# Second block's attentions: two PSUM banks in turn for the background products, one for the weighted sum over the keys

## The chip, the cores and the metric
The program runs on one core of one Trainium2 chip. The metric is the device time of one execution in microseconds (us); a profiled execution gives the trace from which rows are shown. The core has five engines that run their own instruction lists side by side and wait for each other by semaphores: TensorE (PE; its weight loads are listed as PEld), VectorE (DVE), ScalarE (ACT), GpSimd (POOL) and SyncE (SP, which issues the DMAs). Matmul results go to PSUM, which has eight banks of 128 x 512 float32; a bank can be written anew only when its last result has been copied out.

## The reference, cut to what matters
Two transformer blocks run one after the other over 512 tokens of width 1024. The second block has three branches, each an attention, gated and then merged:

```
q_a, k_a, v_a, ..., z_a, ..., gate_logits = split(h @ w_in)
o_a = top-k sparse causal attention   (8 heads of 64, 128 keys per query)
o_b = causal attention                (8 heads, 96 wide scores, 64 wide values)
o_m = attention over 256 memory rows  (4 heads of 128)
ys     = stack([o_a * silu(z_a), o_b * silu(z_b), o_m * silu(z_m)])
branch = einsum('nbsw,nwd->nbsd', ys, w_branch)
merged = einsum('bsnd,nbsd->bsd', sigmoid(gate_logits), branch)
x      = x + merged @ w_out
```

An attention is: scores = q k^T, softmax over the keys, then the sum over the keys of probability times value. z and the gate logits need only h, not the attention, so their products can run beside it.

## The kernel before, in words
Every float32 product of h or an activation with a weight tile is made of three 128x128 by 128x512 matmuls on high and low parts (`product`, lines 403 to 405). A weight tile (1024 x 128) is loaded by SP, its high part is written by ACT (`split_high`, L356), its low part by POOL (`split_low`, L365).

The kernel is a row of stages with a barrier between them. In the second block each branch makes a `Background` object (line 544): a list of jobs, one weight tile and one 128 x 512 output each (4 jobs for z, 8 for the gate, in the sparse branch 5 more for the latent branch's input). A job has 8 steps of 3 matmuls, so 24 matmuls. `Background.pe(pe, n)` puts the next n steps into PE's list, wherever a stage calls it; `Background.act` puts the copy of a finished job (`take`, L583) and the high part of a later weight tile (L356) into ACT's list, at the point where the next job begins. At a job's first step PE waits for its weight tile and, if an earlier job used the same bank, for that job's copy (`background_taken`). `bank(i)` names the bank: bank 7 for every job that begins inside another stage; the jobs from number `alone` on, which run by themselves in the stage after the attention (`finish`), take banks 0 to 6 in turn.

The background is called in these stages of the second block:
- `select_keys` (sparse branch; the top-k choice): after the last of 13 rotations PE does 36 background steps, 4 jobs and a half. The rotations use banks 4, 5 and 6 in turn; the last step of a rotation is ACT's copy L3075 (semaphore `rotated`).
- `rotate_tiles` (latent branch): one step after each of 16 rotations, whose banks are 0 to 3.
- `attend` (all three branches; line 2283): one step in each unit.

`attend` goes through units, one for each head and each 128 queries: 32 units in the sparse and in the latent attention (8 heads of 4, with 128, 256, 384 and 512 keys), 16 in the memory attention (4 heads of 4, 256 keys each). PE's list in unit i: the scores of unit i (L2307, banks 0 to 2), one background step (L403 to L405), the transposes of the probabilities of unit i-3 (L2318, banks 3 and 4), and, where i-4 is the last unit of a head, that head's weighted sum over the keys (L2332: 10 matmuls with causal keys, 8 of them in a row of the trace, 8 for the memory attention). The sum was put in bank 5 or 6 by the head's number. DVE scales, masks and takes the maximum (L2349, L2352) and divides by the sum (L2362, L2363); ACT takes the exponential (L2376), does its background part (L583, L356), copies the transposed probabilities (L2387) and a head's finished sum (L2394), in this order. The first block's attention calls `attend` too, with two value parts in banks 5 and 6 and no background.

Background jobs begin at units 4, 12, 20 and 28 of the sparse attention, at units 0, 8, 16 and 24 of the latent one, and at units 0 and 8 of the memory one.

Of the kernel before, what the change touches and what calls it, by code (L numbers as in the profile page):

```python
# [27 lines left out]
S = 512  # L28
# [515 lines left out]
class Background:  # L544
# [10 lines left out]

    def bank(self, i):

        return (i - self.alone) % 7 if i >= self.alone else 7

    def pe(self, pe, steps):  # L560
        k = self.k
# [1721 lines left out]
def attend(k, units, scale, background=Idle(), pace=0):  # L2283


    nc, G = k.nc, k.counter
    n = len(units)
    scored, maxed, expd, scaled = G("score_ready"), G("max_ready"), G("exp_ready"), G("prob_ready")
    turned, copied, summed, taken = G("turned_ready"), G("turned_taken"), G("sum_ready"), G("out_taken")
    NS, NB = 4, 3  # L2290
    TURN, SUM = 3, 4
    with ExitStack() as ctx:
        s = k.sbuf(ctx, k.fresh("scores"), [P, NS, S])
        pT = k.sbuf(ctx, k.fresh("probT"), [P, 2, max(un.keys for un in units) // P, S])
        small = k.sbuf(ctx, k.fresh("row_stats"), [P, NS, 4])

        with k.stage() as block:
            @block.tensor
            def _(pe):
                for i in range(n + SUM):  # L2300
                    if i < n:
                        un = units[i]
                        if i >= NB:

                            pe.wait_ge(*expd.ge(i - NB + 1))
                        for j, (q, key) in enumerate(un.pairs):
                            last = nc.tensor.matmul(k.banks[i % NB][:, 0:un.keys], q, key, start=(j == 0),  # L2307
                                                    stop=(j == len(un.pairs) - 1))
                        last.then_inc(*scored.inc())
                        background.pe(pe, pace)  # L2310
                    if 0 <= i - TURN < n:
                        m, un = i - TURN, units[i - TURN]

                        pe.wait_ge(*scaled.ge(m + 1))
                        if m >= 2:
                            pe.wait_ge(*copied.ge(m - 1))
                        for c in range(0, un.keys, P):
                            last = nc.tensor.transpose(k.banks[3 + m % 2][:, c:c + P], s[:, m % NS, c:c + P], k.const("ident"))  # L2318
                        last.then_inc(*turned.inc())
                    if 0 <= i - SUM and (i - SUM) % ST == ST - 1:  # L2320
                        m, h, un = i - SUM, (i - SUM) // ST, units[i - SUM]

                        pe.wait_ge(*copied.ge(m + 1))
                        heads = 2 // len(un.value)
                        if h >= heads:
                            pe.wait_ge(*taken.ge(h - heads + 1))
                        rows = slice(un.row, un.row + un.width)
                        for part, value in enumerate(un.value):
                            for c in range(un.keys // P):

                                q0 = 0 if un.mask is None else c * P
                                last = nc.tensor.matmul(k.banks[5 + (h % 2 if heads == 2 else part)][rows, q0:S], value(c),  # L2332
                                                        pT[:, h % 2, c, q0:S], start=(c == 0), stop=(c == un.keys // P - 1))
                        last.then_inc(*summed.inc())

            @block.vector
            def _(dve):
                chain = Chain(dve, G("dve_step"))
                for i in range(n + 1):
                    if i < n:  # L2340
                        un = units[i]
                        st = small[:, i % NS, :]
                        dve.wait_ge(*scored.ge(i + 1))
                        src = k.banks[i % NB][:, 0:un.keys]
                        if un.mask is not None:
                            if i >= NS:

                                dve.wait_ge(*turned.ge(i - NS + 1))
                            chain(nc.vector.scalar_tensor_tensor(out=s[:, i % NS, 0:un.keys], in0=src,  # L2349
                                                                 scalar=scale if un.scale is None else un.scale,  # L2350
                                                                 in1=un.mask, op0=ALU.mult, op1=ALU.add))
                            nc.vector.tensor_reduce(st[:, 1:2], s[:, i % NS, 0:un.keys], AX, ALU.max,  # L2352
                                                    negate=True).then_inc(*maxed.inc())
                        else:
                            chain(nc.vector.tensor_reduce(st[:, 0:1], src, AX, ALU.max))
                            nc.vector.tensor_scalar(st[:, 1:2], st[:, 0:1], -scale, None, ALU.mult).then_inc(*maxed.inc())
                    if i:
                        m, un = i - 1, units[i - 1]
                        st = small[:, m % NS, :]

                        dve.wait_ge(*expd.ge(m + 1))
                        chain(nc.vector.reciprocal(st[:, 3:4], st[:, 2:3]))  # L2362
                        nc.vector.tensor_scalar(s[:, m % NS, 0:un.keys], s[:, m % NS, 0:un.keys], st[:, 3:4], None,  # L2363
                                                ALU.mult).then_inc(*scaled.inc())

            @block.scalar
            def _(act):
                for i in range(n + SUM):
                    if i < n:
                        un = units[i]  # L2370

                        act.wait_ge(*maxed.ge(i + 1))
                        if i >= NS:
                            act.wait_ge(*turned.ge(i - NS + 1))
                        src = s[:, i % NS, 0:un.keys] if un.mask is not None else k.banks[i % NB][:, 0:un.keys]
                        nc.scalar.activation(s[:, i % NS, 0:un.keys], src, ACT.Exp, bias=small[:, i % NS, 1:2],  # L2376
                                             scale=1.0 if un.mask is not None else scale,
                                             accum_out=small[:, i % NS, 2:3]).then_inc(*expd.inc())
                        background.act(act, pace)
                    if 0 <= i - TURN < n:  # L2380
                        m, un = i - TURN, units[i - TURN]
                        h, t = m // ST, m % ST

                        act.wait_ge(*turned.ge(m + 1))
                        if h >= 2:
                            act.wait_ge(*summed.ge(h - 1))
                        nc.scalar.copy(pT[:, h % 2, 0:un.keys // P, t * P:(t + 1) * P],  # L2387
                                       k.banks[3 + m % 2][:, 0:un.keys].rearrange("p (c q) -> p c q", q=P)).then_inc(*copied.inc())
                    if 0 <= i - SUM and (i - SUM) % ST == ST - 1:
                        h, un = (i - SUM) // ST, units[i - SUM]  # L2390

                        act.wait_ge(*summed.ge(h + 1))
                        rows = slice(un.row, un.row + un.width)
                        nc.scalar.copy(un.out, k.banks[5 + h % 2][rows, :] if len(un.value) == 1 else  # L2394
                                       k.psum[:, 5:7, :]).then_inc(*taken.inc())

            @block.gpsimd
            def _(pool):
                k.split_low(pool, k.split_h)

            @block.sync
            def _(sp):
                k.prefetch_split(sp)
# [641 lines left out]
def select_keys(k, qk, qi, ki, wi, wiT, v, chosen, cos, sin, y, sg, gained_matrix, q_scale, background, fill):  # L3045

    nc, G = k.nc, k.counter
    norms_ctx = ExitStack()
    with norms_ctx, ExitStack() as ctx:
# [3 lines left out]
                      S, 2, room=sg, kept=(4, q_scale[:], AHD ** -0.5), sum_bank=3)  # L3053
        matrix, gained_cos = k.const("rotate_a"), sg[:, 7, :]

        items = [(x, matrix, cos) for x in (ki[:], *(qi[:, t, :] for t in range(4)))]
# [74 lines left out]
        with k.stage() as block:  # L3131
            @block.tensor
            def _(pe):
                for t in range(ST):
                    last = nc.tensor.matmul(k.banks[3][:, t * AH:(t + 1) * AH], wiT[:, t * P:(t + 1) * P],
                                            k.const("ident", AH)[:, 0:AH], start=True, stop=True)
# [16 lines left out]
                for i in range(FIRST, len(items)):  # L3153
                    fill.pe(pe, 4)
                    pe_rotate(pe, i)
                background.pe(pe, CHOOSE_STEPS)

            @block.scalar
# [538 lines left out]
```

## Time and profile before

| | us |
|---|---|
| Median of 3 runs | 1895.54 |
| Lowest and highest run | 1889.73, 1901.23 |
| The profiled execution | 1900.23 |
| Its span (first to last instruction) | 1898.4 |
| PE busy in it | 1746.5 (92%) |
| DVE, ACT, POOL busy | 880.0, 708.8, 726.5 |
| Mean granted TensorE clock | 0.946 of full speed |
| Sparse attention (stage) | 1227.05 to about 1345.5 |
| Latent attention | 1513.3 to about 1598 |
| Memory attention | 1732.4 to about 1768 |

The span is one execution's clock, from its first instruction; the profiled execution's time is 1.8 us more. A view by windows cuts the span at chosen times and gives each engine's busy time in each piece and PEclk, the clock that TensorE was granted: 1.00 is 2.4 GHz, 0.50 is 1.2 GHz, and a value between is a mixture over the piece. A timeline row is one instruction, or several alike in a row; in square brackets stands how long the engine had been idle before it and what ended the idle time.

### The profile page before, as it was taken

How to read it: one execution, taken by the hardware profiler on the slowest of the kernel's cores; microseconds unless marked ns; L12 is line 12 of the kernel's file. 1: busy time of each engine (PE TensorE's matmuls, PEld its weight loads, DVE VectorE, ACT ScalarE, POOL GpSimd, SP SyncE). 2: the span in 40 equal slices, each digit the busy share in tenths (PEclk: the TensorE clock that was granted, in tenths of full speed). 3: DMA queues.
4: the chain of work that ended last, by engine and by line, in shares of the span. 5: the costliest groups of instructions: out<-in, count | busy, mean ns of one | idle time of the engine just before them, and what ended most of it. 6: DMA issues, size and time to landing. Idle time of an engine off the chain costs nothing. (4 is left out here: it accounts for less than half of the span.)

```text
span 1898.4 us, 25330 instructions
## 1 busy us (share of the span) xinstructions
PE 1746.5 (92%) x10334; PEld 1305.1 (69%) x10334; DVE 880.0 (46%) x1448; ACT 708.8 (37%) x1195; POOL 726.5 (38%) x375
## 2 busy tenths in 40 slices
PE   5999998889998999999999997899998799987989
PEld 4866668858785878888788854644674466774777
DVE  4647884448524355333212938634142864314231
ACT  4334452234424432222233432334345155334431
POOL 5423433316440445555444543300244612452342
PEclk9999999879999999999999998967898899998999
DMA  4311120014320223322233311200113010341131
GB/s 165 136 56 56 56 68 4 4 57 123 107 93 23 89 78 101 100 89 94 84 101 106 132 45 34 67 22 14 43 53 109 23 34 17 128 139 60 51 106 56
DMA packets 39571, 138.55 MB, mean 73 GB/s; under 512 B 4384, under 2 KB 5664, under 8 KB 38304
## 3 DMA queue, kind: packets, MB, share of 16 engines
q1 hardware_dynamic: 39456, 136.93, 22.1%
q8 instruction: 82, 1.34, 0.3%
q14 instruction: 33, 0.27, 0.0%
HBM read 132.72 MB, written 4.19 MB: 72 GB/s over the span
## 5 line engine op out<-in xcount | busy, mean ns | idle before, releaser
L365 POOL TENSOR_TENSOR parts<-ring,parts 128x1024 fp32r<-128x1024 f32 (+3 forms) x251 | 572.4, 2285 | 962.1 <-ACT parts L356 961.6
L403 PE MATMUL banks<-h_hi,parts 128*128 128x512 f32 x1096 | 472.4, 431 | 30.2 <-ACT a_gate L583 8.3
L404 PE MATMUL banks<-h_lo,parts 128*128 128x512 f32 x1096 | 438.6, 400 | 0.0
L405 PE MATMUL banks<-h_hi,parts 128*128 128x512 f32 x1096 | 438.4, 400 | 0.0
L356 ACT CAST parts<-ring 128x1024 fp32r<-128x1024 f32 (+3 forms) x251 | 244.7, 979 | 195.2 <-PE banks L405 189.2
L403 PEld LDWEIGHTS banks<-h_hi,parts 128*128 128x128 f32 x1096 | 209.9, 192 | 115.3 <-issue 62.1
L404 PEld LDWEIGHTS banks<-h_lo,parts 128*128 128x128 f32 x1096 | 210.7, 192 | 54.4 <-issue 9.6
L405 PEld LDWEIGHTS banks<-h_hi,parts 128*128 128x128 f32 x1096 | 210.0, 192 | 50.1
L2729 ACT CAST ffn_act_hi<-ffn_gate 128x512 fp32r<-128x512 f32 x22 | 13.7, 623 | 167.0 <-DVE ffn_gate L2628 167.0
L2685 DVE TENSOR_TENSOR ffn_raw<-banks,ffn_root 128x512 f32<-128x512 f32 x22 | 15.2, 691 | 125.5 <-PE banks L405 125.4
L403 PE MATMUL banks<-ffn_act_hi,parts 128*128 128x512 f32 x176 | 69.1, 393 | 3.2 <-DVE ffn_gate L2628 3.2
L405 PE MATMUL banks<-ffn_act_hi,parts 128*128 128x512 f32 x176 | 69.2, 393 | 0.0
L404 PE MATMUL banks<-ffn_act_lo,parts 128*128 128x512 f32 x176 | 69.1, 393 | 0.0
L2376 ACT ACTIVATE scores<-scores,row_stats 128x128 f32<-128x128 f32 (+1 forms) x64 | 35.9, 562 | 78.8 <-DVE row_stats L2352 78.5
L2349 DVE SCALAR_TENSOR_TENSOR scores<-banks,a_q_scale,a_chosen 128x128 f32<-128x128 f32 (+3 forms) x32 | 17.6, 550 | 75.6 <-PE banks L2307 75.6
L2695 DVE TENSOR_TENSOR x<-x,banks 128x512 f32<-128x512 f32 x8 | 5.5, 687 | 96.0 <-PE banks L405 96.0
L2318 PE MATMUL banks<-consts,scores 128*128 128x128 f32 x224 | 44.9, 302 | 2.3 <-ACT probT L2387 2.3
L2318 PEld LDWEIGHTS banks<-consts,scores 128*128 128x128 f32 x224 | 33.0, 156 | 16.2 <-issue 6.7
L2387 ACT COPY probT<-banks 128x256 f32<-128x256 f32 (+2 forms) x96 | 37.7, 398 | 11.8 <-PE banks L2318 11.7
L403 PEld LDWEIGHTS banks<-ffn_act_hi,parts 128*128 128x128 f32 x176 | 33.5, 190 | 10.7 <-DVE ffn_gate L2628 3.6
L2363 DVE TENSOR_SCALAR scores<-scores,row_stats 128x256 f32<-128x256 f32 (+2 forms) x96 | 38.8, 404 | 3.4
L1007 DVE SCALAR_TENSOR_TENSOR ffn_gate<-ffn_raw,vecs,ffn_gate 128x511 f32<-128x511 f32 (+1 forms) x44 | 39.0, 887 | 1.6
(556 smaller groups left out, 3159.7 us busy)
## 6 DMA issues: line engine op xcount, KB each, us to landing
ring<-weights SPq DMA_DIRECT2D x211, 512.0 KB, 3.5
ring<-weights SPq DMA_DIRECT2D x24, 256.0 KB, 2.5
ring<-weights SPq DMA_DIRECT2D x8, 384.0 KB, 3.1
x<-xT SPq DMA_DIRECT2D x2, 1024.0 KB, 6.1
x<-xT SPq DMA_DIRECT2D x1, 2048.0 KB, 7.7
x_spill<-x SPq DMA_DIRECT2D x2, 1024.0 KB, 4.8
x<-x_spill SPq DMA_DIRECT2D x1, 2048.0 KB, 7.7
outT<-x SPq DMA_DIRECT2D x8, 256.0 KB, 2.0
```

What stands on the lines that cost most here:

```text
L356: self.nc.scalar.copy(self.parts[:, t % PARTS, 0, 0:w], self.ring[:, t % SLOTS, 0:w]).then_inc(self.high_ready, 1)
L365: self.nc.gpsimd.tensor_tensor(self.parts[:, t % PARTS, 1, 0:w], self.ring[:, t % SLOTS, 0:w], self.parts[:, t % PARTS, 0, 0:w].bitcast(F3 ...
L403: nc.tensor.matmul(out, w.hi, x.hi, start=first, stop=False)
L404: nc.tensor.matmul(out, w.hi, x.lo, start=False, stop=False)
L405: return nc.tensor.matmul(out, w.lo, x.hi, start=False, stop=last)
L1007: ins = nc.vector.scalar_tensor_tensor(out=dst[:, lag:S], in0=bank[:, 0:S - lag], scalar=k.vec(f"{weights}{j}", tile), in1=dst[:, lag:S], ...
L2318: last = nc.tensor.transpose(k.banks[3 + m % 2][:, c:c + P], s[:, m % NS, c:c + P], k.const("ident"))
L2349: chain(nc.vector.scalar_tensor_tensor(out=s[:, i % NS, 0:un.keys], in0=src, scalar=scale if un.scale is None else un.scale, in1=un.mask, ...
L2363: nc.vector.tensor_scalar(s[:, m % NS, 0:un.keys], s[:, m % NS, 0:un.keys], st[:, 3:4], None, ALU.mult).then_inc(*scaled.inc())
L2376: nc.scalar.activation(s[:, i % NS, 0:un.keys], src, ACT.Exp, bias=small[:, i % NS, 1:2], scale=1.0 if un.mask is not None else scale, acc ...
L2387: nc.scalar.copy(pT[:, h % 2, 0:un.keys // P, t * P:(t + 1) * P], k.banks[3 + m % 2][:, 0:un.keys].rearrange("p (c q) -> p c q", q=P)).the ...
L2685: nc.vector.tensor_tensor(r, bank(gate_job(f)), root, ALU.mult).then_inc(*G("gate_taken").inc())
```

## The change
Three edits:
- Background jobs that begin inside another stage alternate between banks 6 (even jobs) and 7 (odd jobs); the jobs that run alone take banks 0 to 5 in turn.
- The weighted sum of one-value attentions always goes to bank 5, so from head 1 on it waits for the copy of the head just before; for the first block's attention with two parts the banks and the wait stay as they were.
- In `select_keys` PE waits, ahead of the background, for 12 rotations to have been copied, since item 11 was in bank 6.

```diff
@@ class Background
     def bank(self, i):
-        return (i - self.alone) % 7 if i >= self.alone else 7
+        return (i - self.alone) % 6 if i >= self.alone else 6 + i % 2
@@ attend, PE
                         pe.wait_ge(*copied.ge(m + 1))
-                        heads = 2 // len(un.value)
-                        if h >= heads:
-                            pe.wait_ge(*taken.ge(h - heads + 1))
+                        if h:
+                            pe.wait_ge(*taken.ge(h))
...
-                                last = nc.tensor.matmul(k.banks[5 + (h % 2 if heads == 2 else part)][rows, q0:S], value(c),
+                                last = nc.tensor.matmul(k.banks[5 + part][rows, q0:S], value(c),
@@ attend, ACT
-                        nc.scalar.copy(un.out, k.banks[5 + h % 2][rows, :] if len(un.value) == 1 else
+                        nc.scalar.copy(un.out, k.banks[5][rows, :] if len(un.value) == 1 else
@@ select_keys, PE
                 for i in range(FIRST, len(items)):
                     fill.pe(pe, 4)
                     pe_rotate(pe, i)
+
+                pe.wait_ge(*G("rotated").ge(len(items) - 1))
                 background.pe(pe, CHOOSE_STEPS)
```

No instruction moves on any engine; only banks and waits differ. PE's list in `select_keys`, at the end of the last rotation (L3069, L3071, in the changed kernel L3068, L3070) and the first background step, before:

```order
L3069 MATMUL banks<-a_y,consts 128x512 [waits rotated,sin_taken]
L3071 MATMUL banks<-a_y,consts 128x512 [waits cos_ready]
L403 MATMUL banks<-h_hi,parts 128x512 [waits low_ready]
L404 MATMUL banks<-h_lo,parts 128x512
L405 MATMUL banks<-h_hi,parts 128x512
```

and now:

```order
L3068 MATMUL banks<-a_y,consts 128x512 [waits rotated,sin_taken]
L3070 MATMUL banks<-a_y,consts 128x512 [waits cos_ready]
L403 MATMUL banks<-h_hi,parts 128x512 [waits low_ready,rotated]
L404 MATMUL banks<-h_lo,parts 128x512
L405 MATMUL banks<-h_hi,parts 128x512
```

The first background matmul has gained the wait on the rotations' copies. In the same stage PE goes from job 0 to job 1, before:

```order
L404 MATMUL banks<-h_lo,parts 128x512
L405 MATMUL banks<-h_hi,parts 128x512
L403 MATMUL banks<-h_hi,parts 128x512 [waits background_taken,low_ready]
L404 MATMUL banks<-h_lo,parts 128x512
L405 MATMUL banks<-h_hi,parts 128x512
```

and now:

```order
L404 MATMUL banks<-h_lo,parts 128x512
L405 MATMUL banks<-h_hi,parts 128x512
L403 MATMUL banks<-h_hi,parts 128x512 [waits low_ready]
L404 MATMUL banks<-h_lo,parts 128x512
L405 MATMUL banks<-h_hi,parts 128x512
```

Job 1 waits for no copy any more; from job 2 on the wait is still there, but for the copy of the job two back, not of the one just finished. In the sparse attention, where the sum of head 1 is followed by unit 12 and a new job begins, the changed kernel has on PE:

```order
L2331 MATMUL banks<-probT_11028,a_v 64x512 [waits out_taken,turned_taken]
L2331 MATMUL banks<-probT_11028,a_v 64x384
L2331 MATMUL banks<-probT_11028,a_v 64x256
L2331 MATMUL banks<-probT_11028,a_v 64x128
L2307 MATMUL banks<-x 128x128 [waits exp_ready]
L403 MATMUL banks<-h_hi,parts 128x512 [waits background_taken,low_ready]
L404 MATMUL banks<-h_lo,parts 128x512
```

These rows read alike in the kernel before (with L2332); what differs is the count that `out_taken` and `background_taken` must have reached.

## Rows read from the trace of the kernel before

**Rows 1.** Who waited for whom: PE, 1150 to 1900 us (total, times, longest).
```profile
PE banks L403 <- ACT a_gate L583: 8.3, 4, 2.3
PE banks L403 <- ACT b_z L583: 5.6, 3, 1.9
...
PE banks L403 <- ACT a_z L583: 3.1, 4, 0.8
...
PE banks L403 <- ACT m_z L583: 1.9, 1, 1.9
```

**Rows 2.** Windows, one each head of the sparse attention; PEclk is third from the end.
```profile
1227.05:1233.63 6.58, 6.58 (x21) 3.23 (x21) 4.35 (x12) 3.05 (x7) 0.00 (x0) 1.00 0.22 80
1233.63:1253.77 20.14, 17.80 (x39) 8.90 (x38) 6.95 (x19) 6.58 (x17) 2.35 (x1) 0.58 0.08 26
1253.77:1263.67 9.90, 9.90 (x39) 5.46 (x38) 5.98 (x16) 4.47 (x13) 0.00 (x0) 1.00 0.01 2
1263.67:1281.88 18.21, 16.22 (x39) 8.11 (x38) 5.97 (x16) 6.31 (x15) 2.36 (x1) 0.63 0.09 29
...
1291.79:1311.63 19.84, 17.85 (x39) 8.88 (x38) 5.97 (x16) 6.31 (x15) 2.35 (x1) 0.57 0.08 27
...
1321.55:1339.78 18.23, 16.24 (x39) 8.14 (x39) 6.62 (x18) 6.31 (x15) 2.36 (x1) 0.63 0.09 29
```

**Rows 3.** Timeline of PE at unit 12 of the sparse attention.
```profile
1266.15 0.47 PE L403 MATMUL banks<-h_hi,parts 128*128 128x512 f32 x1 [1.99 <-ACT a_gate L583]
```

**Rows 4.** Timeline of ACT at the same place.
```profile
1263.78 0.58 ACT L2394 COPY a_y<-banks 64x512 f32<-64x512 f32 x1 [0.82 <-PE banks L2332]
1264.90 0.40 ACT L2376 ACTIVATE scores<-scores,row_stats 128x128 f32<-128x128 f32 x1 [0.54 <-DVE row_stats L2352]
...
1265.42 0.58 ACT L583 COPY a_gate<-banks 128x512 f32<-128x512 f32 x1
1265.90 1.05 ACT L356 CAST parts<-ring 128x1024 fp32r<-128x1024 f32 x1
```

**Rows 5.** Windows, one each head, of the latent attention.
```profile
1513.32:1522.58 9.26, 7.40 (x21) 5.33 (x22) 3.98 (x11) 4.47 (x9) 2.36 (x1) 0.66 0.38 114
...
1531.08:1541.70 10.62, 8.77 (x39) 5.60 (x38) 6.32 (x16) 5.98 (x15) 2.37 (x1) 1.00 0.16 50
1541.70:1550.23 8.53, 8.53 (x39) 5.53 (x39) 5.97 (x16) 4.56 (x13) 0.00 (x0) 1.00 0.00 0
1550.23:1562.50 12.27, 10.41 (x39) 6.71 (x39) 6.11 (x16) 6.08 (x15) 2.37 (x1) 0.86 0.12 43
```

**Rows 6.** Timeline of PE at the start of the latent attention.
```profile
1513.32 0.77 PE L2307 MATMUL banks<-b_k,x 96*128 96x128 f32 x2 [8.22 <-PEq L287]
1515.94 0.77 PE L403 MATMUL banks<-h_hi,parts 128*128 128x512 f32 x1 [1.85 <-ACT b_z L583]
```

**Rows 7.** Timeline of PE at unit 8 of the memory attention.
```profile
1749.48 0.47 PE L403 MATMUL banks<-h_hi,parts 128*128 128x512 f32 x1 [1.87 <-ACT m_z L583]
```

**Rows 8.** Window from unit 8's scores to unit 9's, memory attention.
```profile
1747.02:1750.47 3.45, 1.58 (x9) 1.03 (x8) 1.00 (x4) 2.57 (x5) 0.11 (x1) 1.00 0.00 0
```

**Rows 9.** Timeline of PE in the stage of the top-k choice.
```profile
1169.97 1.12 PE L3071 MATMUL banks<-a_y,consts 128*128 128x512 f32 x2 [2.14 <-POOL a_y L3092]
...
1216.49 0.47 PE L403 MATMUL banks<-h_hi,parts 128*128 128x512 f32 x1 [0.77 <-ACT a_z L583]
...
1222.97 0.47 PE L403 MATMUL banks<-h_hi,parts 128*128 128x512 f32 x1 [0.77 <-ACT a_z L583]
...
1227.05 0.46 PE L2307 MATMUL banks<-x 64*128 64x128 f32 x2 [1.08 <-PEq L287]
```

**Rows 10.** Timeline of ACT there.
```profile
1192.88 0.59 ACT L3075 COPY x<-banks 128x512 f32<-128x512 f32 x1 [4.89 <-PE banks L3071]
```

**Rows 11.** Timeline of POOL there.
```profile
1223.85 2.40 POOL L365 TENSOR_TENSOR parts<-ring,parts 128x1024 fp32r<-128x1024 f32 x1 [4.08 <-ACT parts L356]
```

## The prediction
> **What bounds the kernel now.** I read the view of waits first, for PE alone, because PE is busy for 92% of the span. Between 1150 and 1900 us thirteen of PE's waits end with ACT's copy of a background job (L583), 20.7 us together [rows 1] (the thirteenth, for b_gate, reads like the one for m_z): four in the top-k stage, four in the sparse attention, four in the latent one (three for b_z, one for b_gate), one in the memory one. The only other idle time of PE between 1227 and 1340 us is the 1.1 us at the barrier. So PE sets the length of the attentions, and the copy is its one obstacle.
>
> Then I cut the sparse attention into heads by windows [rows 2]. Heads without a job boundary take 9.9 us with PE busy throughout at PEclk 1.00 (1253.77 is shown; 1281.88 and 1311.63 read 9.91 and 9.92). The four heads with a boundary take 20.14, 18.21, 19.84 and 18.23 us, though they issue the same 39 matmuls, and their PEclk is 0.57 to 0.63. Only about 2 us of the difference is the pause itself. The rest is the clock: right after each of these four pauses TensorE goes from 2.4 to 1.2 GHz and stays there for most of the head. In the latent attention [rows 5] a head without a boundary takes 8.53 us, one whose pause did not lower the clock 10.62, one whose pause did 12.27 (two of these). So the wait is worth much more than 20.7 us, and what matters is whether PE has no pause at all at a boundary, not whether it is shorter.
>
> How the pause comes about [rows 3, 4]: PE issues the scores of unit 12 at 1263.67 [rows 2], and its next instruction, a new job's first matmul, waits for bank 7. ACT can copy bank 7 only in its own order: behind the head's sum (L2394) and behind unit 12's exponential (1264.90), which itself needs the scores that PE has just made and DVE's two operations on them. The copy starts at 1265.42, PE goes on at 1266.15.
>
> **The change part by part.**
>
> *Two banks for the jobs, in the attentions.* The new job goes to the other bank, whose last job was copied 8 units earlier, so the wait is met. The weight tile is ready too, as its parts are made three jobs ahead. Pause and clock loss both go. Sparse attention: each such head becomes one of 9.91 us, (20.14 + 18.21 + 19.84 + 18.23) - 4 x 9.91 = 36.8 us, of which the pauses are 2.34 + 3 x 1.99 = 8.3 us and the clock 28.5 us. Latent attention: 10.62 - 8.53 = 2.1 for head 2, 2 x (12.27 - 8.53) = 7.5 for heads 4 and 6. Its head 0 starts at 1.2 GHz, because PE has been idle for 8.22 us at the barrier [rows 6]; there 1.85 us of pause goes at least, and if the whole head ran at full clock it would be like the sparse head 0 scaled by 8.53/9.91, so 5.7 us instead of 9.26, 3.6 at most. I take 2.5, nearer to the pause, since the idle time at the barrier stays. Together 12.1 us. Memory attention: the pause is 1.87 us, and the clock did not fall (PEclk 1.00) [rows 8]. Its units are short (3.45 us from score to score with the pause, 1.6 without) [rows 7, 8], so ACT's extra work at a boundary, 0.58 + 1.05 us [rows 4], may hold up a later transposition or sum: between 0.9 and 1.87 us, and I take 1.7.
>
> *What is late next.* ACT and DVE. In a boundary head ACT is busy for 6.31 us and DVE for 5.97, against PE's 9.9; in the latent attention 6.1 and 6.3 against 8.5. ACT's 1.6 us block is taken between the exponential of unit i and the copy for unit i-3, which PE needs two units later, over 4 us in these attentions. I see no new wait there, but allow 0.1 us for each of nine boundaries, 0.9 us.
>
> *One bank for the sums.* The sum of head h now waits for the copy of head h-1. On ACT that copy stands three units ahead of the last copy of transposed probabilities, for which the sum waits anyway, so the wait is always met: 0. In rows 4 the copy of a sum is over at 1264.36; the next sum comes a head later.
>
> *Six banks instead of seven in the stages behind.* A job there waits for the copy of the job six back. 24 matmuls take about 5.7 us (6.48 us between 1216.49 and 1222.97, less 0.77) [rows 9], so five whole jobs, some 28 us, lie between: 0.
>
> *The top-k stage.* The added wait is for a copy that was over at 1193.5 [rows 10], while by the spacing of the jobs the first one began at 1216.49 - 3 x 6.48 + 0.77 = 1197.8 [rows 9]: 0. Four pauses of 0.77 us go. The stage ends with POOL (1226.25) [rows 11], whose last tile can be split only once job 3 has ended, and that is behind three of the pauses: 3 x 0.77 = 2.3 us. PE itself is done 3.1 us earlier and so waits longer at the barrier: 1.08 + 0.77 = 1.85 us instead of 1.08 [rows 9].
>
> *The sum.* 36.8 + 12.1 + 1.7 + 2.3 - 0.9 = 52.0 us. From the profiled execution's 1900.2 us that gives 1848.2. The median of the runs is 4.7 us lower than that execution; one pause more or less that lowers the clock is worth 6 to 8 us, so I take that difference for pauses that other executions got through at full clock. These are gone in any case, and I don't take it off: 1848.
>
> [...] PE idle time at a bank hand-over is what rows 2 and 5 show as the cause of the lowered clock, by its timing. [...]
>
> **The rivals.**
>
> *A, the wait moves.* PE passes the boundary and stops at the next transposes or sum for ACT's block. For it: ACT is a chain in fixed order. Against it: the slack worked out above, and no wait on L2318 or L2332 in the two longer attentions before their last units. The clock would fall as before, and only the top-k stage and head 0 of the latent attention would gain: 1900.2 - 2.3 - 1.9 = 1896.
>
> *B, the pauses go but the clock falls all the same,* because attention matmuls (64 or 96 rows, transposes) keep TensorE little occupied. For it: the clock takes most of a head to come back in the sparse attention. Against it: four falls in four boundary heads, none in the three heads between, nor in head 0. Gain: 8.3 + 4 x 1.85 + 1.9 + 2.3 = 19.9, so 1880.
>
> *C, the barrier takes over one fall.* PE's idle time ahead of the sparse attention grows to 1.85 us, as long as the pauses of the latent attention, of which two of the three that came at full clock lowered it; against it, idle times of 2.14 us [rows 9] and 1.87 [rows 7] did not. The attention would start at 1.2 GHz, and a boundary head shows the price, 17.80 - 9.91 = 7.9 us, if it lasts as long: 1856; a shorter fall, as in head 0 of the latent attention, costs about 3 us.
>
> *D, slower.* The clock falls at that same barrier and never comes back, because at 1.2 GHz PE does not get over what is wanted, and nothing interrupts the attention any more. Each head at 1.2 GHz costs 7.9 us against a free one. The gain of 52 us is used up from the seventh head at 1.2 GHz on. All eight sparse heads: 7 x 17.80 + 6.58 x 1.8 = 136.4 us instead of 112.7, so 1900.2 + 23.7 - 2.3 - 12.1 - 1.7 = 1908, and more if the latent attention goes the same way. Against it: the clock came back within every boundary head of both attentions.
>
> *E, the change doesn't do what it says:* a second bank doesn't free PE, as the tile's readiness was the real wait. Speaks against it: the copy ends 0.15 us before PE's matmul (1266.00 and 1266.15) [rows 3, 4]. About 1900.
>
> **How the numbers follow.** My forecast 62%, C 20%, B 8%, A 5%, D 3%, E 2%. 1848 us is the likeliest; by itself it lies between 1841 (latent head 0 in full, 1.1, and further falls of the clock in later stages that come or go by chance, some 6) and 1856. With C it is 1840 to 1866, the upper end for C together with some of the unknown costs; B, A, D and E, 18%, are left out. A measurement of this kernel tells a change from none at about 0.5%, 9.5 us. Faster than that: forecast, B, C and a part of A, 92%; the same: most of A and E, 5%; slower: 3%.
>
> **What would show it.** No PE wait on L583 from 1150 us on; eight sparse heads with PEclk 1.00 and 9.9 us each but for the first (6.6); latent heads of 8.5 us, the first one near 7; the sparse attention some 37 us shorter; L2331 without a wait on ACT's copy of the sum; POOL still last in the top-k stage, PE's idle time behind it 1.85 us. I am wrong if boundary heads still read PEclk near 0.6, if L2318 or L2331 show waits of over 1 us in mid-attention, or if head 0 of the sparse attention reads 0.5.

## The result and the profile after

The changed kernel takes 1845.62 us (median of 4 runs, 1844.01 to 1848.04) against 1896.82 us for the kernel before on the same chip: a ratio of 0.9735, 95% interval 0.9702 to 0.9767. (A fourth run of the kernel before, 1898.10 us, has joined the three of the table above.) The forecast was 1848 us. The profiled execution took 1846.14 us with a span of 1844.3.

Who waited for whom, PE, in the second block of the changed kernel (total, times, longest); the two longest and the two that stand for the attentions:

```profile
PE banks L403 <- PEq L287: 13.2, 9, 3.9
PE banks L2307 <- PEq L287: 11.6, 3, 8.5
...
PE banks L2331 <- ACT probT L2386: 1.8, 3, 0.7
...
PE banks L2318 <- ACT probT L2386: 1.3, 3, 0.6
```

No line says any more that PE waits for L583: all thirteen waits of [rows 1] are gone. The waits on L2331 and L2318 are three each as before, at the last units of the attentions, where no background is left to fill them. What remains is the barrier (L287) and other stages.

The windows of the sparse attention's heads, to be read against [rows 2]:

```profile
1222.59:1229.19 6.60, 6.60 (x21) 3.23 (x22) 4.37 (x12) 3.05 (x7) 0.00 (x0) 1.00 0.26 79
1229.19:1239.12 9.93, 9.93 (x39) 5.44 (x39) 7.15 (x19) 6.16 (x17) 2.38 (x1) 1.00 0.17 53
1239.12:1249.03 9.91, 9.91 (x39) 5.43 (x38) 5.98 (x16) 4.46 (x13) 0.00 (x0) 1.00 0.01 2
1249.03:1258.95 9.92, 9.92 (x40) 5.44 (x39) 5.97 (x16) 5.89 (x15) 2.45 (x1) 1.00 0.16 53
```

The next three read alike (9.91 to 9.92 us); the last head with the tail behind it takes 15.60 us instead of 23.92. A head with a job boundary (ACT 6.16 and 5.89 us busy) and one without (4.46) now take the same 9.91 to 9.93 us, PE is busy all the time, and PEclk is 1.00 from end to end. 20.14 us have become 9.93 without one instruction less.

The latent attention's first heads, against [rows 5]:

```profile
1471.95:1479.95 8.00, 8.00 (x21) 5.75 (x22) 5.56 (x11) 4.46 (x9) 2.36 (x1) 0.62 0.27 91
1479.95:1488.46 8.51, 8.51 (x40) 5.44 (x38) 7.05 (x20) 4.83 (x15) 0.00 (x0) 1.00 0.09 34
1488.46:1497.00 8.54, 8.54 (x39) 5.54 (x38) 6.41 (x16) 5.77 (x15) 2.37 (x1) 1.00 0.20 60
```

Heads 2, 4 and 6 have lost pause and clock fall (8.54 instead of 10.62 and 12.27). Head 0 still begins at 1.2 GHz behind the long barrier and takes 8.00 instead of 9.26.

Where the time went, from the windows by stage of both traces (each from PE's first instruction in the stage to its first in the next):

| stage | before | after | difference |
|---|---|---|---|
| all before the top-k stage | 1108.13 | 1104.87 | -3.3 |
| top-k stage up to the last rotation | 88.15 | 90.12 | +2.0 |
| last rotation to the sparse attention | 30.77 | 27.60 | -3.2 |
| sparse attention | 118.42 | 81.70 | -36.7 |
| latent attention | 84.22 | 73.51 | -10.7 |
| memory attention | 35.92 | 33.93 | -2.0 |
| the three parts between and behind | 432.8 | 432.6 | -0.2 |

The first two rows lie ahead of the first changed wait. Their 1.3 us is one execution against another, no gain of the change. In the second row lies a pause of PE of 2.14 us, a wait for POOL: the clock fell behind it in the changed kernel's profiled execution and not in the one before [rows 9]. Over all thirteen profiled executions of this document it fell there in eleven. The four rows in the middle make 52.6 us; the forecast's terms made 52.0.

### The profile page after: what moved, and what is told of

Its sections match the earlier page's. It is cut to its first block and busy times, and to the rows that moved or that the text cites. A ratio compares the mean times of both kernels' runs of the same rounds, so it can differ in the third digit from the quotient of the medians.

```text
span 1844.3 us, 25333 instructions
## 1 busy us (share of the span) xinstructions
PE 1708.2 (93%) x10334; PEld 1287.6 (70%) x10334; DVE 883.9 (48%) x1448; ACT 706.2 (38%) x1195; POOL 726.7 (39%) x375
## 5 line engine op out<-in xcount | busy, mean ns | idle before, releaser
L2318 PE MATMUL banks<-consts,scores 128*128 128x128 f32 x224 | 39.6, 273 | 2.3 <-ACT probT L2386 2.3
L403 PEld LDWEIGHTS banks<-ffn_act_hi,parts 128*128 128x128 f32 x176 | 33.0, 188 | 10.4 <-DVE ffn_gate L2627 3.6
L2318 PEld LDWEIGHTS banks<-consts,scores 128*128 128x128 f32 x224 | 29.2, 140 | 14.2 <-issue 4.1
L405 PEld LDWEIGHTS banks<-ffn_act_hi,parts 128*128 128x128 f32 x176 | 33.0, 188 | 7.0
```

Of the source, the lines that this page charges most:

```text
L403: nc.tensor.matmul(out, w.hi, x.hi, start=first, stop=False)
L405: return nc.tensor.matmul(out, w.lo, x.hi, start=False, stop=last)
```

## The experiments

Each ratio is against the kernel before, run beside it on the same chip; times of two different experiments can come from two chips. "The two banks" is short for background jobs alternating between banks 6 and 7.

**The banks without the freedom from the wait.** In the changed kernel:

```diff
                 before = [j for j in range(i) if self.bank(j) == self.bank(i)]
+                if i and i < self.alone:
+                    before = [i - 1]
```

> Changed kernel, banks as there (6 and 7 in turn, sums in bank 5), but a job that begins inside another stage waits again for the copy of the job just before it. Theory (the pause at the boundary, and the clock it lowers, is the whole gain; the bank number as such does nothing): back to the kernel before, ratio 0.995 to 1.005, some 1890 to 1901 us, boundary heads of the sparse attention at 18 to 20 us with PEclk about 0.6. Rival (putting the jobs and the sums into other banks helps by itself, or the single waits elsewhere do): a good part of the 51 us stays, 1850 to 1880 us.

Measured: 1889.0 us, ratio 0.9985 (0.9961 to 1.0009). Every wait is back as in [rows 1], and so are the heads:

```profile
1231.92:1250.45 18.53, 16.19 (x39) 8.17 (x38) 6.95 (x19) 6.58 (x17) 2.35 (x1) 0.63 0.10 28
1250.45:1260.34 9.89, 9.89 (x40) 5.44 (x39) 5.97 (x16) 4.45 (x13) 0.00 (x0) 1.00 0.01 2
1260.34:1280.06 19.72, 17.73 (x39) 8.90 (x38) 5.97 (x16) 6.31 (x15) 2.35 (x1) 0.57 0.09 27
```

So the other banks do nothing by themselves that can be told (at most 0.4% by the interval): the gain is the wait.

**The three side edits alone.** `bank` gives 7 again for jobs inside other stages; one bank for the sums, six for the later jobs and the wait on the rotations stay.

> Changed kernel, but background jobs keep bank 7 everywhere: only the sums in one bank, the six banks of the later stages and the wait on the rotations remain. Theory (all three are free): ratio to the kernel before 0.995 to 1.005. Rival (the sum's wait or the seventh bank costs): 1 us a head for the sums, so over 1905 us, or waits on the sums' copies in the trace.

Measured: 1898.16 us, ratio 1.001 (0.9985 to 1.0035). They cost nothing that can be told, and the trace has the waits of the kernel before, none on a sum's copy.

**The two banks in the sparse branch alone.**

```diff
-        return (i - self.alone) % 6 if i >= self.alone else 6 + i % 2
+        return (i - self.alone) % 6 if i >= self.alone else 6 + i % 2 if len(self.jobs) == 17 else 7
```

> Changed kernel, but only the sparse branch's jobs alternate; the latent and the memory branch's jobs keep bank 7. Theory (each attention's gain is its own sum of pauses and clock): the latent attention's 12.1 and the memory attention's 1.7 us are lost, so 1845.6 + 13.8 = 1859 us, 1854 to 1863. Rival (the gain is made mostly in one place by chance falls of the clock, or a shift of one stage changes the next): under 1850 or over 1868 us.

Measured: 1858.65 us (1857.88 to 1862.19), ratio 0.9812 (0.9787 to 0.9836). 13.0 us of the gain are lost by the two medians (14.6 by the two ratios), where the latent and the memory attention had measured 12.7 in the two traces. So the gains add up by stage.

**Filling the pause.** The old wait is back, but PE works during it:

```diff
+                if i and i < self.alone:
+                    hi, lo = k.slot(t)
+                    for r in range(3):
+                        product(k, k.banks[self.bank(i)], Halves(hi[:, 0:P], lo[:, 0:P]), k.h[:, 0, :], True, True)
+                    pe.wait_ge(k.background_taken, self.taken + i)
```

> Changed kernel with the old wait at each boundary, but ahead of it PE does nine throw-away matmuls of 128x512 (three products of the new job's first tile) into the free bank, some 2.1 us in which it used to stand idle. The computation is otherwise the same. Theory (the idle time lowers the clock, and not the boundary as such): PEclk stays 1.00, each boundary costs some 2.1 us and no more: 9 in the attentions and 3 on the top-k stage's way, 1845.6 + 25 = 1871 us. Rival (the clock falls for another reason at a boundary, such as the wait itself or DMA of the next tile): as the kernel before, 1895 us or more.

Measured: 1869.6 us (1867.21 to 1872.29), ratio 0.9873 (0.9837 to 0.991). Two heads of its sparse attention, with and without a boundary:

```profile
1260.97:1272.91 11.94, 11.94 (x48) 7.12 (x48) 6.13 (x16) 6.09 (x15) 2.37 (x1) 1.00 0.15 44
1272.91:1282.81 9.90, 9.90 (x39) 5.43 (x38) 5.98 (x16) 4.46 (x13) 0.00 (x0) 1.00 0.01 3
```

The boundary head costs 2.0 us more, the nine matmuls' time, and PEclk is 1.00 in every head of the sparse attention and in every latent head but the first, which starts at 1.2 GHz behind the barrier. With the same wait, the same bank to be copied and the same tile loads, the clock holds if PE works through the wait. So idle time is the cause of the fall, and throw-away work in its place is worth some 20 us against the bare wait (1869.6 us against 1889.0).

**The same pause at one boundary alone.** `before = [i - 1]` only for job 6 of the sparse branch (unit 12).

> Changed kernel, with the old wait at one boundary alone, unit 12 of the sparse attention. Theory (pause 2.0 us plus a clock fall of 6 to 8 us): one head of 18 to 20 us with PEclk about 0.6, the others at 9.9, in all +8 to +10 us, 1855 us. If that execution gets through the pause at full clock: +2 us, 1848. Rival (the clock's state feeds on itself, so one fall brings others): over 1865 us.

Measured: 1852.47 us (1848.51 to 1853.75), ratio 0.9784 (0.9753 to 0.9815). The profiled execution (1848.5) went another way than either:

```profile
1218.88:1229.14 10.26, 10.26 (x22) 4.57 (x22) 5.10 (x14) 3.22 (x8) 0.00 (x0) 0.60 0.18 51
1229.14:1239.97 10.83, 10.83 (x40) 6.08 (x39) 7.65 (x17) 6.08 (x17) 2.38 (x1) 0.90 0.17 48
...
1249.88:1261.80 11.92, 9.93 (x39) 5.43 (x38) 6.17 (x16) 6.08 (x15) 2.38 (x1) 1.00 0.14 44
```

The pause at unit 12, 1.99 us, cost just its length: this time the clock did not fall. But it fell at the barrier ahead of the attention, where PE was idle for 2.09 us, and the first two heads took 4.6 us longer for it. The other three executions, 3.4 to 5.2 us longer, have no trace, so where their time went isn't known. A pause of 2 us is thus a risk of a fall and no certainty, and one fall does not bring the next.

**A shorter pause in the old kernel.** One bank, all as before, but at a boundary ACT copies the finished job ahead of the exponential:

```diff
                         un = units[i]
+                        early = isinstance(background, Background) and background.begins()
+                        if early:
+                            background.take(act, background.act_at // DT - 1)
 
                         act.wait_ge(*maxed.ge(i + 1))
...
```

(The cut part keeps `act` from taking the same copy a second time.)

> Kernel before (one bank), but in the attentions ACT copies the finished job ahead of the exponential of the boundary unit, not behind it. PE's pause shrinks from 2.0 to some 0.8 us (scores until the copy is over) and does not vanish. Theory as my prediction put it (what matters is whether there is a pause at all): the clock falls about as often, only some 9 x 1.1 = 10 us are won, 1885 us. Rival (a short pause leaves the clock alone): 1.1 us plus the clock's part of 28 + 5 us are won, so 1896 - 10 - 33 = 1853 us, with PEclk 1.00 in all sparse heads.

Measured: 1865.26 us (1864.51 to 1866.34), ratio 0.9845 (0.9817 to 0.9872). The rows of PE at the first two boundaries of the sparse attention and the windows of their heads:

```profile
1234.14 0.47 PE L403 MATMUL banks<-h_hi,parts 128*128 128x512 f32 x1 [1.72 <-ACT a_gate L583]
1261.23 0.47 PE L403 MATMUL banks<-h_hi,parts 128*128 128x512 f32 x1 [0.95 <-ACT a_gate L583]
```

```profile
1231.94:1249.88 17.94, 16.22 (x39) 8.13 (x38) 7.00 (x19) 6.48 (x17) 2.36 (x1) 0.62 0.10 29
...
1259.79:1270.68 10.89, 9.94 (x40) 5.44 (x39) 6.58 (x16) 5.97 (x15) 2.37 (x1) 1.00 0.16 48
```

The pause of 1.72 us lowered the clock; the pauses of 0.95, 0.96 and 0.96 us of the sparse attention and of 0.82 us of the latent one did not. The time lies between the 1885 us of the theory and the 1853 of the rival, since the first pause was 1.72 us and not 0.8. The order of two ACT instructions gives more than half of the change's gain by the ratios (1.55% of 2.65%), with no second bank.

**A pause without a bank.** In the changed kernel:

```diff
+                        if isinstance(background, Background) and background.pe_at and background.pe_at % DT == 0:
+                            pe.wait_ge(*expd.ge(i + 1))
                         background.pe(pe, pace)
```

> Changed kernel, but at each job boundary in the attentions PE waits for the exponential of the unit whose scores it has just issued. This puts a pause of about 1.3 us (DVE 0.35 + 0.29, ACT 0.40 and the way between) in place of the 2.0 us of the kernel before, with no bank involved. Theory (a pause of PE lowers the clock whatever its cause, from some length between 0.8 and 2 us on): 9 x 1.3 = 12 us for the pauses if the clock holds, 1858 us; with 6 to 8 us for each fall, up to 1890 us. Rival (the falls need the copy out of the bank, or the write into another bank): PEclk 1.00 throughout and 1845 to 1850 us.

Measured: 1868.86 us (1864.07 to 1886.31), ratio 0.989 (0.9834 to 0.9947). From the profiled execution (1871.65):

```profile
1214.36:1226.00 11.64, 11.64 (x22) 5.31 (x22) 5.11 (x14) 3.23 (x8) 0.00 (x0) 0.52 0.14 45
...
1252.27:1269.86 17.59, 16.30 (x40) 8.10 (x39) 6.80 (x16) 6.22 (x15) 2.38 (x1) 0.61 0.10 30
...
1509.31:1519.69 10.38, 8.89 (x40) 5.62 (x39) 6.72 (x16) 5.87 (x15) 2.40 (x1) 1.00 0.18 51
```

Pauses of 1.29 us with no copy and no bank involved can lower the clock too: at two of the three boundaries of the sparse attention that PE reached at 2.4 GHz, at none of the latent one. In this execution the clock fell at the barrier as well (first row, 6.60 us in the changed kernel).

**Ending the top-k stage earlier.** `CHOOSE_STEPS` 32 instead of 36.

> Changed kernel, but 32 instead of 36 background steps in the top-k stage, so that it ends with job 3 whole and without the weight tile that is split behind it. PE, not POOL, ends the stage, and PE's idle time ahead of the sparse attention goes from 2.1 to about 1 us; the 4 steps (2.8 us) move into the stage where jobs run alone. Theory: the attention starts 3.9 us earlier, 2.8 us are given back, so 1 us faster, 1844.5. Rival (the jobs' boundaries, now at units 0, 8, 16 and 24, fall in with the sums and bring new waits): 2 us or more slower.

Measured: 1844.60 us (1842.45 to 1846.81), ratio 0.9746 (0.9716 to 0.9776): no difference from the changed kernel that can be told. The stage did end earlier (attention from 1218.82 us instead of 1222.59, PE idle 0.32 us at the barrier), but boundary heads take 10.35 us, since ACT's work at a boundary now falls in the units ahead of a head's sum:

```profile
1243.38 2.37 PE L2331 MATMUL banks<-probT,a_v 128*64 128x512 f32 x8 [0.36 <-ACT probT L2386]
```

**Versions that go further.** Low parts that POOL makes at a stage's end are left to the next stage, in the top-k stage the last one, then in the rotation stage of the latent branch all:

```diff
@@ select_keys, POOL
-                k.split_low(pool, k.split_h)
+                k.split_low(pool, k.split_h - 1)
@@ rotate_tiles, POOL (second version only)
-                k.split_low(pool, k.split_h)
```

> The changed kernel once more, unchanged, as the measure for the two runs beside it: 1843 to 1849 us. Its profile shows whether the clock falls at the barrier ahead of the sparse attention in this execution: by the idle time of 2.1 us there, some executions should have it (first head 10 us with PEclk about 0.6, as in the run with one old wait), others not (6.6 us).

> Changed kernel, but POOL makes the low part of the last weight tile of the top-k stage only in the sparse attention's stage (it is needed three jobs later). PE ends the stage instead of POOL. Theory: PE's idle time at that barrier goes from 2.1 to about 1.1 us and the clock can't fall there any more: 1 us, plus 4.6 us times the share of executions in which it falls now: 1843.5 us. Rival (the low part is then late, or contends with DVE in the first head): no gain, 1846.

> The same, and in the latent branch's rotation stage POOL makes no low parts at all; the next stage makes them. In the changed kernel POOL's two low parts (5.1 us) run beside DVE's last additions, which then take 2.8 us for two and 4.7 for one instead of 1.2 each. Theory (these additions are slowed by POOL's work, and DVE ends the stage): some 3 to 5 us less for that stage, 1840 us. Rival (the slow additions are POOL's last rotations' doing, and the low parts are only moved onto the attention): 1843 to 1846.

Measured, beside each other: the changed kernel again 1847.68 us (1846.65 to 1851.19), ratio 0.9759 (0.9735 to 0.9782); the first version 1842.08, ratio 0.9721 (0.9697 to 0.9745); the second 1838.97 (1838.17 to 1842.84), ratio 0.9710 (0.9687 to 0.9734). The intervals of the second version and of the changed kernel just don't overlap; those of the first and of the changed kernel do, and the two versions can't be told apart. PE's first instruction in the sparse and in the latent attention of the second version:

```profile
1219.89 0.46 PE L2307 MATMUL banks<-x 64*128 64x128 f32 x2 [0.30 <-PEq L287]
...
1465.55 0.46 PE L2307 MATMUL banks<-b_k,x 96*128 96x128 f32 x2 [3.81 <-PEq L287]
```

The barrier ahead of the sparse attention is down from 2.09 us to 0.30, so the fall that hit two of the other profiled executions there has hardly a pause to start from; the repeated changed kernel, idle for 2.09 us there, didn't show the fall. The one ahead of the latent attention is down from 8.54 to 3.81 us. DVE's last additions in the rotation stage of the changed kernel (1465.40 to 1470.48 us POOL makes two low parts):

```profile
1461.92 1.16 DVE L3023 TENSOR_TENSOR b_k<-b_k,turned_half 96x512 f32<-96x512 f32 x1
...
1463.61 4.67 DVE L3023 TENSOR_TENSOR b_k<-b_k,turned_half 96x512 f32<-96x512 f32 x1
...
1468.81 2.83 DVE L3023 TENSOR_TENSOR b_k<-b_k,turned_half 96x512 f32<-96x512 f32 x2
```

and the last of the second version, without POOL's low parts:

```profile
1463.48 1.75 DVE L3023 TENSOR_TENSOR b_k<-b_k,turned_half 96x512 f32<-96x512 f32 x2
```

Beside POOL's rotations (L3035, until 1465.43 in the changed kernel, until 1464.08 in the version) an addition takes 1.16 us. POOL's rotations stand in both kernels and the slow additions in one, so they come with the low parts; the expectation's rival is out. The addition of 4.67 us began 1.8 us before the first low part, so how much of it each of POOL's operations held up isn't shown. The heads 0 and 1 of the latent attention, in which POOL now makes these parts, take 16.16 us together, against 16.51 in the changed kernel and 16.52 in the first version, which makes the parts where the changed kernel does: what was moved costs nothing there that can be seen.

## Why the prediction was right

The forecast was made from the profiled execution: 1900.2 us less 52.0. The two profiled executions differ by 54.1 us, the medians by 51.2. The terms' errors, up to 1.4 us each, partly cancel, and that the sum (52.6 measured in these stages) came out closer than they did is luck.

- *What bounds.* PE sets the length of the attentions, and its wait for the copy was the obstacle: right. With the wait alone put back, the old time is back.
- *The clock term,* 28.5 of the 36.8 us in the sparse attention: right in mechanism and size (36.7 measured). The filled pause shows that the idle time lowered the clock, not the boundary.
- *Latent attention,* 12.1 us forecast, 10.7 measured. The term that was mis-sized is its head 0, 2.5 us forecast and 1.26 measured. From the two PEclk values (0.66 of 9.26 us, 0.62 of 8.00) the time at 1.2 GHz was 6.3 us before and 6.1 now. The head leaves the low clock as late as before, and part of the pause of 1.85 us had cost nothing: without it PE only does more of its work at 1.2 GHz. The sign "the first one near 7" failed by the same: it read 8.00.
- *Memory attention,* 1.7 forecast, 2.0 measured; the allowance for ACT's block, there and 0.9 us over all boundaries, was not needed.
- *Top-k stage,* 2.3 forecast, 3.2 measured: 3 x 1.04 and not 3 x 0.77. Jobs now start 5.44 us apart instead of 6.48. A timeline row gives a matmul 0.39 us, but the next one starts 0.23 us after it, so an idle time that is counted from a row's end is some 0.2 us too short. PE's idle time at the barrier became 2.09 us by the same, not 1.85.
- *One bank for the sums, six banks, the added wait:* 0 each, as measured together. The start of the first job was worked out 1 us too late (1197.8 us; no pause stands ahead of that job, and its row begins at 1196.74), still 3 us behind the copy that it waits for.
- *"What matters is whether PE has no pause at all, not whether it is shorter":* wrong. A shortened pause wins more than half of the gain. PE's pauses at full clock in the profiled executions, by length, and how often 1.2 GHz followed:

| pause, us | where | clock fell |
|---|---|---|
| 0.82 to 0.96 | boundaries of the sparse and latent attention, early copy | 0 of 6 |
| 1.29 | the same, wait for the exponential | 2 of 6 |
| 1.72 | the same, first boundary of the early copy | 1 of 1 |
| 1.85 to 2.34 | the same, five kernels with the old wait | 22 of 25 |
| 1.87 | boundary of the memory attention, four kernels | 0 of 4 |
| 2.09 | barrier ahead of the sparse attention | 2 of 5 |
| 2.14 or 2.15 | a rotation in the top-k stage | 11 of 13 |

- *Rivals A, B and E* did not occur. *Rival C* is real: of the five profiled executions in which PE was idle for 2.1 us at that barrier, those of the runs with one old wait and with the wait for the exponential had the fall, the two of the changed kernel and the one of the sparse-only run did not. It cost 4.6 us where nothing else followed, between the 3 and 7.9 us forecast. The pause of 2.14 us that was held against it was one of the two of thirteen behind which the clock stayed. That C did not come in the measured profile is thus in part luck. *Rival D* did not occur, though in the run that waits for the exponential the clock stayed at 1.2 GHz for 24 us after the barrier, with a pause on the way.
- The Trainium skill, "TensorE: Matmul & The Clock Gate", section "HAM oscillation — how this bites in real kernels", reports that adding PSUM double-buffering gave no further gain, of a kernel whose loops had already been rearranged to keep TensorE busy. Here the second bank gave 51 us, because it ended a wait that left PE idle. The Trainium skill, same page, section "A second HAM failure mode: psum-queue depth-cycling", reports short idle times between groups of matmuls and an oscillating clock in a kernel that cycles through banks. Here passing between banks did not make the clock oscillate once the wait was gone: PEclk is 1.00 in all of the changed kernel's sparse heads. What the first of these two sections of the Trainium skill says of idle PE and a lowered clock agrees with the filled pause; it tells it of waits for a DMA, and here waits for a copy or an exponential did the same.

Still open: why a pause of 2 us lowers the clock in one execution and not in the next, why the memory attention's boundary bears 1.87 us, and why the latent attention bears 1.3 us better than the sparse one. The runs show the frequencies, no more.

## What to carry to other kernels

Price a wait of TensorE by windows around it, with the granted clock, not by its length: here 20.7 us of waits were worth 51 us, as pauses of 2 us were followed by up to 17 us at half clock. Where one result bank hands over between jobs, give the next job a bank that has been free for long, or at least put the copy first in the copying engine's order. If a wait can't be removed, shorten it, here to below 1 us, or work through it: even throw-away matmuls paid. That held for single pauses with busy stretches around them. Ahead of the memory attention PE waits 1.69, 0.51, 0.94, 0.24 and 0.93 us with 0.3 to 1.9 us of matmuls between, and in the changed kernel's trace the clock is down (PEclk 0.50 from 1679.50 us) before the last of these waits ends at 1680.37.

## What the runs showed of the hardware

- The clock can take far longer to come back than it takes to fall. It was down within 1.3 us of the end of the pauses shown here. Windows of the kernel before, behind two pauses in the sparse attention and one in the latent:

```profile
1236.30:1253.40 17.10, 16.94 (x34) 8.46 (x35) 4.78 (x12) 4.67 (x12) 2.35 (x1) 0.50 0.09 31
1267.10:1280.70 13.60, 13.60 (x28) 6.49 (x27) 4.77 (x12) 3.71 (x10) 2.29 (x1) 0.50 0.12 39
1553.80:1557.20 3.40, 3.40 (x11) 2.50 (x9) 1.40 (x4) 1.41 (x4) 2.02 (x1) 0.50 0.06 23
```

The pauses ended at 1236.46, 1266.15 and 1552.57 us. From then on PE is busy throughout, and still at 1.2 GHz for 13.6 to 17.1 us in the one attention, for 3.4 us in the other.
- The same pause of 1.99 us at the same place (unit 12 of the sparse attention) lowered the clock in the profiled execution of the kernel before and left it alone in that of the run with one old wait.
- DVE additions of 96x512 took 1.16 us beside POOL's rotations (96x512) and up to 4.67 us when POOL's low parts (128x1024) ran beside a part of them. Moving two low parts, 5.1 us of POOL's work, to the next stage cut PE's idle time at that barrier by 4.7 us (8.54 to 3.81).
